# Pairwise addition of RMS-norm squares on VectorE, four square buffers, and norm steps spread over the output projection

## The chip, the cores and the metric

The kernel runs on the eight cores of one Trainium2 chip, each with two of the sixteen sequences and its own copy of the weights. No core waits for another. The metric is the device time in microseconds of the slowest core. The engines are named as in the profile: PE (TensorE, matmuls), DVE (VectorE), ACT (ScalarE), POOL (GpSimd) and SP (SyncE, which here only issues DMAs). PEld is PE's weight load.

## What is computed

A two-layer trunk on x of shape 16 x 2048 x 1024. Each layer has an RMS norm, a joint input projection to three causal mixers, an output projection with a residual addition, a second RMS norm and a SwiGLU feed-forward network (FFN). One more RMS norm ends the trunk.

```python
def rms_norm(x, g):                      # cut to what matters
    y = x * rsqrt(mean(x * x, axis=-1, keepdims=True) + 1e-6)
    return y * g

for l in range(2):
    h = rms_norm(x, norm1_g[l])
    z = h @ w_in[l]                       # 1024 -> 1792
    ya = conformer_conv(z[..., :768])     # gate, causal conv of 31, layer norm, silu, pointwise
    yb = spatial_gating(z[..., 768:1536]) # gelu, layer norm, 128x128 mixing in chunks of 128
    yc = multiscale_pool(z[..., 1536:])   # trailing means over 2, 4, 8, 16
    x = x + concat(ya, yb, yc) @ w_out[l]
    h = rms_norm(x, norm2_g[l])
    gate, up = split(h @ w_gate_up[l])    # 2 x 2816
    x = x + (silu(gate) * up) @ w_down[l]
return rms_norm(x, final_g)
```

## The kernel before

x lies transposed in SBUF for the whole sequence, as `xT`: 128 channels by 8 blocks k, by 2048 positions in float32. Work goes in four tiles j of 512 positions. Each core runs sequence 0, layers 0 and 1, then sequence 1, layers 0 and 1. For each layer: input projection `A` (8 groups of 8 matmuls a tile, results to DRAM `yd` and back as `y2`), `conv`, the gating and pooling parts, `PW` (pointwise projection, 3 groups of 3 matmuls a tile), `WO` (output projection, 8 groups of 8 matmuls a tile, each followed by a residual addition on DVE) and the `FFN`. The FFN works in four chunks of the hidden size; after gate and up groups come down groups, in the last chunk 4 matmuls each, tile after tile, with a residual addition on DVE behind each group (line 990).

**The norms.** There are 40: `r1` before the input projection (16), `r2` before the FFN (16), `rF` at the end (8). `norm_closures` (line 534) makes a list of small steps for one norm of one tile. Step k squares block k on ACT (`sq`) into one of two 16-bit buffers `sqr`, and issues for block k-2 four matmuls of `sqr` against a column of ones (`stat`), which sum over the channels into 4 columns of one PSUM bank. For `r1` it also makes `xb`, the scaled 16-bit copy, on DVE for even k and on ACT for odd k (`mkxb`). The last step, `fin`, reads the bank on DVE and takes the power -0.5 on POOL. After `r2`, `bcast_closures` spreads the result over the partitions (`dia` on DVE, one matmul) and eight DVE operations write `h2T`.

**What sets the order.** Each engine runs its queue in the order in which the program issues instructions. `push` puts a step into a queue `bg`, `tick(n)` takes n steps out of it, and `need(tag)` takes steps out until the tagged one is done. Ticks stand behind groups of matmuls: 1 behind each down group of the last chunk and each group of `A`, 5 behind each group of `WO`, 1 behind each of `PW`, 4 behind each gate or up group. `idle(n)` pushes n steps that issue nothing for the norm. At the start of a sequence `x_tr` transposes the input with one tick for each of 8 groups; `fin_store` does the same for the output of the sequence before. In the first sequence `band_consts`, which goes back and forth between POOL and DVE, is issued after the steps of tile 1's norm are pushed and before `A` takes them. In the layer that follows an FFN, the norms of tiles 0 to 2 run beside the last down groups of the next tile and what is left runs in `A`.

**Waits.** `Prog.add` derives waits from the buffers that each instruction names: a write waits for the earlier readers and writers of every buffer whose address range overlaps. `next_bank` gives the 8 PSUM banks in turn and passes over one that has been written and not yet read. From offset `AB` on lies a region of 134336 bytes in which tiles of different stages share addresses; `sgB` (offset 129216, 3072 bytes) holds the gate norm's constants, loaded on SP before `A` of tile 3.

Of the kernel before, what the change touches and what calls it, by code (L numbers as in the profile page):

```python
# [7 lines left out]
BF16 = mybir.dt.bfloat16  # L8
# [178 lines left out]
def build_program(nseq=2, depth=2):  # L187
# [109 lines left out]
    ybt = AT("ybt", 123072, [128, 4, DB], BF16)  # L297
    sgB = AT("sgB", 129216, [128, 2, DB], F32)
    ya = [AT("ya%d" % i, 110784 + 3072 * i, [128, 3, NT], BF16) for i in range(2)]
    cb32 = AT("cb32", 132288, [32, DA], BF16)  # L300
    cbf = AT("cbf", 124608, [32, DA], F32)
    cbr = AT("cbr", 126144, [32, DA], F32)
# [87 lines left out]
    def push(fn, tag=None, q=None):  # L390
        (bg if q is None else q).append((fn, tag))
# [37 lines left out]
    def bxT(k, j):  # L429
        return B("xT", k, j)  # L430
# [7 lines left out]
    def jc(j):  # L438
        return slice(j * NT, (j + 1) * NT)
# [94 lines left out]
    def norm_closures(s, l, j, rt, kind, with_xb):  # L534
        st = {}
        sqs = {}
        br = B("r", kind, j)

        def sq(k):
            i = sq_rr[0] % len(sqr)  # L540
            sq_rr[0] += 1
            sqs[k] = i
            act_op(sqr[i][:], xT[:, k, jc(j)], AF.Square, [bxT(k, j)], [B("sqr", i)])

        def stat(k):
            if k == 0:
                st["bk"], st["bb"] = next_bank()
            bk, bb = st["bk"], st["bb"]
            i = sqs[k]

            def fn(e, bk=bk, i=i, k=k):
                ins = None
                for q in range(4):
                    ins = e.matmul(bk[:, q:q + 1], sqr[i][:, q * 128:(q + 1) * 128], ocS[:, 0:1],  # L554
                                   start=(k == 0 and q == 0), stop=(k == 7), skip_group_check=True)
                return ins
            P.add("tensor", fn, reads=[B("sqr", i), bC], writes=[bb])

        def mkxb(k):
            if k % 2 == 0:  # L560
                ts(xb[j][:, k, :], xT[:, k, jc(j)], pvc(l, PV_G1 + k), None, ALU.mult, None, [bxT(k, j), bPV], [bxb(j, k)])
            else:
                act_op(xb[j][:, k, :], xT[:, k, jc(j)], AF.Copy, [bxT(k, j), bPV], [bxb(j, k)],
                       scale=pvc(l, PV_G1 + k))

        def fin():
            ts(rt[:, 4 * j:4 * j + 4], st["bk"][:, 0:4], RMS_EPS, None, ALU.add, None, [st["bb"]], [br])
            pool(lambda e: e.tensor_tensor(out=rt[:, 4 * j:4 * j + 4], in0=rt[:, 4 * j:4 * j + 4],  # L568
                                           in1=mhalf[:, 0:4], op=ALU.pow), [br, bC], [br])

        def step(k):
            if k >= 2:
                stat(k - 2)
            if k < 8:
                if with_xb:
                    mkxb(k)
                sq(k)
        for k in range(9):
            push(lambda k=k: step(k))

        def last():
            stat(7)
            fin()
        push(last, (kind, s, l, j))

    def idle(n):
        def other():
# [347 lines left out]
    def norm2(s, l, j):  # L935
        norm_closures(s, l, j, r2, "r2", False)
        hold = {}
        idle(5)

        def sink(bk, bb):  # L940
            hold["k"] = (bk, bb)
        bcast_closures(s, l, j, r2, "r2", sink)

        def sc(k):
            bk, bb = hold["k"]
            stt(h2T[j][:, k, :], xT[:, k, jc(j)], pvc(l, PV_G2 + k), bk[:], ALU.mult, ALU.mult,
                [bxT(k, j), bb, bPV], [bh2(j, k)])
        for k in range(8):
            push(lambda k=k: sc(k), ("h2", s, l, j) if k == 7 else None)
# [233 lines left out]
```

How the kernel before makes its waits and increments, by code:

```python
                def body(eh):  # L165
                    for fn, waits, tok, dma in e.ops:
                        for k, v in waits:
                            eh.wait_ge(sems[k], v)
                        ins = fn(eh)
                        ins.then_inc(sems[tok[0]], 16 if dma else 1)
                    if e.name == "sync":
                        for k, v in finals:
                            eh.wait_ge(sems[k], v)
```

## Time and profile before

| | |
|---|---|
| median of 3 runs | 3058.99 us (3058.8 to 3324.05) |
| profiled execution, slowest core | 3059.71 us |
| span of core 0 (profiled), first to last instruction | 3058.1 us |
| spans of cores 1 to 7 | 3019.6 to 3050.5 us |
| PE busy | 2844.7 us (93%), 15632 matmuls |
| DVE busy | 1207.3 us (39%) |
| ACT busy | 823.5 us (27%) |
| POOL busy | 177.4 us (6%) |
| mean granted PE clock, core 0 | 0.958 |

The profile is that of the slowest core. A busy share is an average over stages with different limits: PE is the bound almost everywhere, and the other engines matter where PE waits for them. In the rows below, a wait in brackets is the idle time of that engine just before the instruction, with what ended it. Matmuls are pipelined, so the busy time of short ones overlaps with that of their neighbours. Idle time of an engine that isn't the bound costs nothing.

### The profile page before, as it was taken

To read this page: it belongs to the slowest core of one execution; us is meant where nothing else is said; L and a number is where in the kernel's file an instruction comes from. 1 tells how busy PE (TensorE), PEld (TensorE's weight loads), DVE (VectorE), ACT (ScalarE), POOL (GpSimd) and SP (SyncE) were. 2 spreads that over 40 slices of the span, in tenths; PEclk is the share of its full clock that TensorE was granted. 3 is DMA by queue.
4 is the path that set the end of the run, shared out by engine and by line. 5 is a ranking of instruction groups with operands and counts; after the bars stand their busy time and mean duration, and the time that the engine had idled before them with its cause. 6 is when DMAs were issued, how large, how long until landed. Compare 5 with 4: busy or idle time off the path is not lost.

```text
span 3058.1 us, 44571 instructions; the slowest of 8 cores (3019.6 to 3058.1 us)
## 1 busy us (share of the span) xinstructions
PE 2844.7 (93%) x15632; PEld 1451.3 (47%) x15632; DVE 1207.3 (39%) x2108; ACT 823.5 (27%) x1356; POOL 177.4 (6%) x286
## 2 busy tenths in 40 slices
PE   5889999999997999999988889999999889999998
PEld 3554344444555444444465544444445544444444
DVE  2372422323554523223354633323335634223236
ACT  3544111010545220110255541010025442110102
POOL 2000000000001010000000001000000000000000
PEclk8887799999998999999998899999999899999999
DMA  8304062220131252221243034221003040222102
GB/s 188 53 1 70 3 94 38 42 32 14 25 53 23 48 83 35 42 36 31 74 151 76 8 63 65 52 42 35 14 15 60 17 69 4 39 41 43 29 21 111
DMA packets 123463, 148.44 MB, mean 49 GB/s; under 512 B 71664, under 2 KB 98416, under 8 KB 121200
## 3 DMA queue, kind: packets, MB, share of 16 engines
q0 software_dynamic: 37376, 100.80, 20.3%
q1 hardware_dynamic: 85872, 44.80, 5.5%
q8 instruction: 131, 2.15, 0.3%
q14 instruction: 84, 0.69, 0.1%
HBM read 219.12 MB, written 23.07 MB: 79 GB/s over the span
## 4 chain that ended last, share of the span: by engine, by line
PE 84%; DVE 6%; issue 4%; ACT 2%; DMA 2%; POOL 1%; SPq 1%; DVEq 0%; ACTq 0%; POOLq 0%
PE bank L332 78%; PE bank L350 2%; PE bank L726 2%; DVE bna L741 1%; ACT sqr L361 1%; PE bank L554 1%; DVE ybt L383 1%; DVE bnv L780 1%; DVE vn L383 1%; PE bank L720 1%; SPq L324 1%; DVE vg L383 1%; DMA yd<-ytok 1%; ACT silT L361 1%; POOL bna L746 1%
## 5 line engine op out<-in xcount | busy, mean ns | idle before, releaser
L332 PE MATMUL bank<-h2T,ring 128*128 128x512 bf16 x5632 | 1227.2, 380 | 0.0
L332 PEld LDWEIGHTS bank<-h2T,ring 128*128 128x128 bf16 x5632 | 551.5, 98 | 667.9 <-issue 22.6
L371 DVE TENSOR_TENSOR xT<-xT,bank 128x512 f32<-128x512 f32 x640 | 438.2, 687 | 506.2 <-PE bank L332 419.3
L332 PE MATMUL bank<-act,wd 128*128 128x512 bf16 x2816 | 618.1, 379 | 7.5 <-DVE r L377 3.7
L371 DVE TENSOR_TENSOR act<-tsil,bank 128x512 bf16<-128x512 f32 x352 | 242.2, 688 | 953.2 <-PE bank L332 945.4
L361 ACT ACTIVATE tsil<-bank 128x512 f32<-128x512 f32 x352 | 210.1, 597 | 1496.6 <-PE bank L332 1483.9
L332 PEld LDWEIGHTS bank<-act,wd 128*128 128x128 bf16 x2816 | 269.9, 98 | 323.4 <-issue 8.0
L361 ACT ACTIVATE sqr<-xT 128x512 bf16<-128x512 f32 x320 | 191.4, 624 | 207.3 <-PE bank L554 194.9
L332 PE MATMUL bank<-w_a_sb,xb 128*128 128x384 bf16 x1024 | 180.1, 336 | 12.9 <-DVE r L377 12.9
L332 PE MATMUL bank<-w_uv_sb,xb 128*128 128x384 bf16 x1024 | 184.0, 343 | 0.0
L332 PEld LDWEIGHTS bank<-w_uv_sb,xb 128*128 128x128 bf16 x1024 | 105.1, 103 | 78.2 <-issue 19.5
L332 PEld LDWEIGHTS bank<-w_a_sb,xb 128*128 128x128 bf16 x1024 | 99.8, 100 | 79.7 <-issue 22.1
L554 PE MATMUL bank<-ocS,sqr 128*128 128x1 bf16 x1280 | 72.4, 164 | 51.7 <-ACT sqr L361 49.5
L554 PEld LDWEIGHTS bank<-ocS,sqr 128*128 128x128 bf16 x1280 | 66.9, 97 | 97.6 <-issue 68.8
L332 PE MATMUL bank<-ybT,wo 128*128 128x512 bf16 x384 | 111.2, 401 | 0.0
L332 PE MATMUL bank<-ya,wo 128*128 128x512 bf16 x384 | 111.1, 401 | 0.0
L324 POOL DMA_DIRECT2D ring<-w_gate_up x88 | 46.7, 534 | 868.3 <-PE bank L332 823.0
L383 DVE SCALAR_TENSOR_TENSOR h2T<-xT,pv,bank 128x512 bf16<-128x512 f32 x128 | 86.6, 741 | 2.4 <-PE bank L332 2.4
L383 DVE SCALAR_TENSOR_TENSOR ytok<-bank,r,sig 128x384 bf16<-128x384 f32 x64 | 39.5, 618 | 119.8 <-PE bank L332 68.5
L332 PE MATMUL bank<-yc,wo 128*128 128x512 bf16 x256 | 81.4, 402 | 0.0
L568 POOL TENSOR_TENSOR r<-r,mhalf 128x4 f32<-128x4 f32 x32 | 32.8, 1024 | 679.0 <-DVE r L377 660.1
L741 DVE BATCH_NORM_STATS2 bna<-xc 128x6 f32<-128x384 f32 x64 | 50.4, 788 | 41.8 <-ACT xc L361 41.8
(123 smaller groups left out, 1762.0 us busy)
## 6 DMA issues: line engine op xcount, KB each, us to landing
ring<-w_gate_up POOLq DMA_DIRECT2D x88, 512.0 KB, 7.4
wd<-w_down POOLq DMA_DIRECT2D x12, 1536.0 KB, 12.1
xst<-x SPq DMA_DIRECT2D x24, 512.0 KB, 6.8
out<-osF SPq DMA_DIRECT2D x16, 512.0 KB, 4.3
w_a_sb<-w_a POOLq DMA_DIRECT2D x8, 768.0 KB, 16.3
w_uv_sb<-w_uv POOLq DMA_DIRECT2D x8, 768.0 KB, 27.0
yd<-ytok SPq DMA_DIRECT2D x16, 384.0 KB, 2.8
y<-yd SPq DMA_DIRECT2D x128, 48.0 KB, 2.9
```

The source lines that it names most:

```text
L324: return P.add(q, lambda e, out=out, in_=in_: e.dma_start(out=out, in_=in_), reads=reads, writes=writes, dma=True, final=final)
L332: ins = e.matmul(out, l, r, start=(first and i == 0), stop=(last and i == n - 1))
L350: ins = e.transpose(out, in_, idn)
L361: return e.activation(out=out, in_=in_, func=func, **kw)
L371: return P.add(eng, lambda e, out=out, in0=in0, in1=in1, op=op: e.tensor_tensor(out=out, in0=in0, in1=in1, op=op), reads=reads, writes=writes)
L383: e.scalar_tensor_tensor(out=out, in0=in0, scalar=scalar, in1=in1, op0=op0, op1=op1),
L554: ins = e.matmul(bk[:, q:q + 1], sqr[i][:, q * 128:(q + 1) * 128], ocS[:, 0:1], start=(k == 0 and q == 0), stop=(k == 7), skip_group_check ...
L568: pool(lambda e: e.tensor_tensor(out=rt[:, 4 * j:4 * j + 4], in0=rt[:, 4 * j:4 * j + 4], in1=mhalf[:, 0:4], op=ALU.pow), [br, bC], [br])
L720: e.matmul(bk[:], onesb[0:32, :], cb32[:, 32 * b:32 * b + 32].unsqueeze(2).to_broadcast([32, 32, TB]), start=True, stop=False, skip_group_ ...
L726: ins = e.matmul(bk[:, gp * 128:(gp + 1) * 128], y2[:, 2 - d:2 - d + NBLK, g], toep[:, g, d].rearrange("p i t -> p (i t)"), start=False, s ...
L741: vec(lambda e: e.bn_stats(out=bna[:, ti, 0:6], in_=xc[:, :, t]), allx, [bst[ti]])
L746: pool(lambda e: e.tensor_tensor(out=bna[:, :, 10], in0=bna[:, :, 10], in1=mhalf[:, 0:4], op=ALU.pow), bst + [bC], bst)
```

## The change

Squares go to four buffers `sqa`, which share addresses with `sgB` (three of them) and lie behind `cb32` (the fourth). For each pair p of blocks a DVE addition `add(p)` sums two square tiles into `sqr[p % 2]`, in 16-bit, and `stat(p)` sends this sum through the ones-column matmuls: 4 groups of four instead of 8 for each norm. A norm has 6 steps instead of 10. Step p issues `stat(p-2)`, then both copies and both squares of pair p, then `add(p-1)`; step 5 issues `stat(3)` and `fin`. For `r2`, an idle step stands behind each of the first five, and `norm2` pushes 4 idle steps instead of 5, so that the number of steps until the broadcast is the same, 15 either way.

```diff
--- before.py
+++ after.py
@@ -297,6 +297,7 @@
     ybt = AT("ybt", 123072, [128, 4, DB], BF16)
     sgB = AT("sgB", 129216, [128, 2, DB], F32)
     ya = [AT("ya%d" % i, 110784 + 3072 * i, [128, 3, NT], BF16) for i in range(2)]
+    sqa = [AT("sqa%d" % i, (129216, 130240, 131264, 133056)[i], [128, NT], BF16) for i in range(4)]
     cb32 = AT("cb32", 132288, [32, DA], BF16)
     cbf = AT("cbf", 124608, [32, DA], F32)
     cbr = AT("cbr", 126144, [32, DA], F32)
@@ -537,24 +538,27 @@
         br = B("r", kind, j)
 
         def sq(k):
-            i = sq_rr[0] % len(sqr)
+            i = sq_rr[0] % len(sqa)
             sq_rr[0] += 1
             sqs[k] = i
-            act_op(sqr[i][:], xT[:, k, jc(j)], AF.Square, [bxT(k, j)], [B("sqr", i)])
-
-        def stat(k):
-            if k == 0:
+            act_op(sqa[i][:], xT[:, k, jc(j)], AF.Square, [bxT(k, j)], [sqa[i].b()])
+
+        def add(p):
+            a, b = sqs[2 * p], sqs[2 * p + 1]
+            tt(sqr[p % 2][:], sqa[a][:], sqa[b][:], ALU.add, [sqa[a].b(), sqa[b].b()], [B("sqr", p % 2)])
+
+        def stat(p):
+            if p == 0:
                 st["bk"], st["bb"] = next_bank()
             bk, bb = st["bk"], st["bb"]
-            i = sqs[k]
-
-            def fn(e, bk=bk, i=i, k=k):
+
+            def fn(e, bk=bk, p=p):
                 ins = None
                 for q in range(4):
-                    ins = e.matmul(bk[:, q:q + 1], sqr[i][:, q * 128:(q + 1) * 128], ocS[:, 0:1],
-                                   start=(k == 0 and q == 0), stop=(k == 7), skip_group_check=True)
+                    ins = e.matmul(bk[:, q:q + 1], sqr[p % 2][:, q * 128:(q + 1) * 128], ocS[:, 0:1],
+                                   start=(p == 0 and q == 0), stop=(p == 3), skip_group_check=True)
                 return ins
-            P.add("tensor", fn, reads=[B("sqr", i), bC], writes=[bb])
+            P.add("tensor", fn, reads=[B("sqr", p % 2), bC], writes=[bb])
 
         def mkxb(k):
             if k % 2 == 0:
@@ -568,20 +572,22 @@
             pool(lambda e: e.tensor_tensor(out=rt[:, 4 * j:4 * j + 4], in0=rt[:, 4 * j:4 * j + 4],
                                            in1=mhalf[:, 0:4], op=ALU.pow), [br, bC], [br])
 
-        def step(k):
-            if k >= 2:
-                stat(k - 2)
-            if k < 8:
-                if with_xb:
-                    mkxb(k)
-                sq(k)
-        for k in range(9):
-            push(lambda k=k: step(k))
-
-        def last():
-            stat(7)
-            fin()
-        push(last, (kind, s, l, j))
+        def step(p):
+            if p >= 2:
+                stat(p - 2)
+            if p < 4:
+                for k in (2 * p, 2 * p + 1):
+                    if with_xb:
+                        mkxb(k)
+                    sq(k)
+            if 1 <= p <= 4:
+                add(p - 1)
+            if p == 5:
+                fin()
+        for p in range(6):
+            push(lambda p=p: step(p), (kind, s, l, j) if p == 5 else None)
+            if kind == "r2" and p < 5:
+                idle(1)
 
     def idle(n):
         def other():
@@ -935,7 +941,7 @@
     def norm2(s, l, j):
         norm_closures(s, l, j, r2, "r2", False)
         hold = {}
-        idle(5)
+        idle(4)
 
         def sink(bk, bb):
             hold["k"] = (bk, bb)
```

## Rows read from the trace of the kernel before

**Rows 1.** the page's chain of work that ended last, shares of the span

```profile
PE 84%; DVE 6%; issue 4%; ACT 2%; DMA 2%; POOL 1%; SPq 1%; DVEq 0%; ACTq 0%; POOLq 0%
```

**Rows 2.** groups by line: engine, what, count | busy us, mean ns | idle

```profile
L371 DVE TENSOR_TENSOR xT<-xT,bank 128x512 f32<-128x512 f32 x640 | 438.2, 687 | 506.2 <-PE bank L332 419.3 <-PE bank L554 86.6
L554 PE MATMUL bank<-ocS,sqr 128*128 128x1 bf16 x1280 | 72.4, 164 | 51.7 <-ACT sqr L361 49.5 <-issue 1.0 <-DVE xT L618 0.6
L361 ACT ACTIVATE sqr<-xT 128x512 bf16<-128x512 f32 x320 | 191.4, 624 | 207.3 <-PE bank L554 194.9 <-DVE xT L371 11.2 <-DVE r L377 1.0
```

**Rows 3.** timeline, FFN end of layer 0: start us, us, engine, what

```profile
789.83 0.24 PE L554 MATMUL bank<-ocS,sqr 128*128 128x1 bf16 x4
...
790.79 0.24 PE L554 MATMUL bank<-ocS,sqr 128*128 128x1 bf16 x4
...
797.75 2.75 PE L332 MATMUL bank<-act,wd 128*128 128x512 bf16 x12 [0.94 <-DVE r L377]
798.88 0.69 DVE L371 TENSOR_TENSOR xT<-xT,bank 128x512 f32<-128x512 f32 x1 [1.28 <-PE bank L332]
799.48 0.48 DVE L377 TENSOR_SCALAR xb<-xT,pv 128x512 bf16<-128x512 f32 x1
799.88 0.68 DVE L371 TENSOR_TENSOR xT<-xT,bank 128x512 f32<-128x512 f32 x1
800.33 0.24 PE L554 MATMUL bank<-ocS,sqr 128*128 128x1 bf16 x4
...
812.87 1.46 PE L332 MATMUL bank<-w_a_sb,xb 128*128 128x384 bf16 x8
```

**Rows 4.** timeline, FFN end of layer 1

```profile
1515.95 2.75 PE L332 MATMUL bank<-act,wd 128*128 128x512 bf16 x12 [0.94 <-DVE rF L377]
```

**Rows 5.** timeline, first sequence, norm of tile 3

```profile
89.31 1.14 ACT L361 ACTIVATE sqr<-xT 128x512 bf16<-128x512 f32 x2
90.35 0.72 ACT L361 ACTIVATE xb<-xT,pv 128x512 bf16<-128x512 f32 x1
...
90.96 0.62 ACT L361 ACTIVATE sqr<-xT 128x512 bf16<-128x512 f32 x1
91.73 0.24 PE L554 MATMUL bank<-ocS,sqr 128*128 128x1 bf16 x4 [0.88 <-ACT sqr L361]
```

**Rows 6.** timeline, output projection of layer 1, first sequence

```profile
1011.95 0.34 PE L554 MATMUL bank<-ocS,sqr 128*128 128x1 bf16 x8
1012.22 0.69 DVE L371 TENSOR_TENSOR xT<-xT,bank 128x512 f32<-128x512 f32 x1 [3.43 <-PE bank L554]
...
1014.29 0.81 PE L332 MATMUL bank<-ya,wo 128*128 128x512 bf16 x3
...
1016.22 0.81 PE L332 MATMUL bank<-ya,wo 128*128 128x512 bf16 x3
...
1049.22 0.34 PE L554 MATMUL bank<-ocS,sqr 128*128 128x1 bf16 x8
...
1054.57 0.81 PE L332 MATMUL bank<-ya,wo 128*128 128x512 bf16 x3
```

**Rows 7.** timeline, input projections with a norm beside them

```profile
821.10 4.06 PE L332 MATMUL bank<-w_a_sb,xb 128*128 128x384 bf16 x24 [0.42 <-DVE r L377]
...
1561.25 0.58 ACT L361 ACTIVATE sig<-bank,r 128x384 f32<-128x384 f32 x1
...
1569.71 0.64 PE L350 MATMUL bank<-identF,xT 128*128 128x128 f32 x4
```

**Rows 8.** timeline, first sequence, tile 1 behind the band constants

```profile
57.88 0.19 DVE L371 TENSOR_TENSOR bandc<-bt,bandc 128x32 bf16<-128x32 f32 x1
...
59.83 0.48 PE L332 MATMUL bank<-w_a_sb,xb 128*128 128x384 bf16 x1 [11.28 <-DVE r L377]
```

**Rows 9.** busy by stretch: stretch, us, PE, PEld, DVE, ACT, POOL, clock, DMA

```profile
1552.00:1562.00 10.00, 9.24 (x47) 7.49 (x48) 3.14 (x7) 3.82 (x6) 1.01 (x1) 0.66 0.35 117
...
1008.00:1016.20 8.20, 6.63 (x57) 3.34 (x56) 1.38 (x2) 5.97 (x11) 0.00 (x0) 1.00 0.74 147
```

## Prediction

> **What bounds the kernel now.** I read the page's chain of work first. PE carries 84% of it [rows 1], so a microsecond taken from PE is a microsecond of the end, and one added in front of PE is too. The other engines count only where PE waits for them. Then the groups of instructions by line: the change works on the squares of the RMS norms, 320 on ACT and 1280 one-column matmuls on PE, four for each square, and there PE waits 49.5 us for ACT [rows 2]. The busy time of those matmuls (72.4 us) overstates them, so I read their price in the timeline. At the end of an FFN a step of the last down projection with a group of four takes 0.96 us from one group of four to the next (789.83 to 790.79); without it three steps take 797.75 to 800.33, 0.86 each [rows 3]. A group of four costs PE 0.10 us.
>
> Three other things are in the timeline. Each norm that goes on beside one matmul group per step leaves a wait "<-DVE r" of 0.94 us: the norm's PSUM bank comes round again just when the norm ends [rows 3, 4]. In the output projection PE stands between two groups (1011.95 to 1014.29), because with two buffers each square waits for an older square's matmuls [rows 6]. And at the start of a sequence the squares are bound by ACT itself: two squares 1.04 us apart from the copy behind them, the copy another 0.61, so 1.65 us a pair [rows 5].
>
> **What the change takes away.** 160 of the 320 groups of four go: 160 x 0.10 = 16 us of PE. The norm holds its bank for four steps instead of eight, so the 0.94 us waits at the FFN ends go too: two at each of four ends, 7.5 us. Four square buffers let ACT run ahead.
>
> **What it adds.** 160 additions on VectorE, and with each a wait: the matmuls of pair p are issued one step after the addition, and the addition stands in DVE's queue behind the residual addition of its step, which waits for that step's PE work. No addition of two 16-bit tiles is in the trace. From below stands the 0.48 us scaling that writes a 16-bit tile of the same shape, whose successor starts 0.40 us later (799.48 to 799.88); from above the 687 ns residual addition from PSUM, whose successor starts 0.60 us later (798.88 to 799.48) [rows 2, 3]. I take 0.48 and 0.40: operands in SBUF and a 16-bit result are nearer to the first; both ends are kept.
> The row nearest by operation is the 687 ns one; the Trainium skill, VectorE: DVE Perf Modes, "The TRN2 errata", gives such a float32 addition (N+151)/0.96, 691 ns at 512, with which that row agrees, and "The perf-mode tier table" lets an addition of 16-bit tiles in SBUF run at twice the rate, which would be an estimate of 424 ns. No row here shows that; by it the whole sum would be 2 us smaller.
>
> **FFN ends of layer 0 (twice).** Count from the end of the down group that pushes the norm. A residual addition starts 0.27 us behind its group's end (1011.95 to 1012.22), the next DVE work 0.60 later, the scaling takes 0.40, the addition 0.48, and PE starts about 0.15 behind its releaser (90.96 + 0.62 to 91.73) [rows 5, 6]. Step 0: residual 0.27, scaling 0.87, free at 1.27. Step 1 (group ends 0.86): residual 1.27, scaling 1.87, addition 2.27 to 2.75. Step 2's group ends at 1.72, but its matmuls can't start before 2.90: PE stands 1.2 us. From there DVE needs 0.60 + 0.40 + 0.40 = 1.40 us a step and PE 0.96, and PE is tied to it: the next three matmul groups start at 4.3, 5.8 and 7.0, waits of 0.4, 0.5 and 0.3. ACT doesn't set this: squares 0 to 3 are done before, squares 4 and 5 start at 2.85 and 6 and 7 end by 6.3, which moves only the last addition. Then three bare steps; eight take 9.7 us. Before, group 2 at 789.83 to the first matmuls of layer 1 at 812.87 gives 23.04 us for 22 steps; with the two before it 24.7 for 24, 8.25 per eight [rows 3]. Three norms: +4.4, two ends: **+8.8**. The 7.5 us of bank waits and half of the groups are already in this.
>
> **FFN ends of layer 1 (twice).** No scaling there, DVE needs 1.00 a step. The same walk gives waits of 0.6, 0, 0.5 and 0 and 8.5 us per eight steps, against the same period before (the wait of 0.94 is there too [rows 4]): 0.25 x 6 = **+1.5**.
>
> **Input projections with a norm beside them.** Before, one square goes with each 8-matmul group (1.35 us, 24 matmuls in 4.06). Now two squares and one scaling, 1.65 us of ACT, fall on one group, with the sigmoid (0.5) between. In layer 0 of the second sequence the first sigmoid, behind the table load, ends at 1561.83, so square 1 ends at 1563.5 and its addition at 1564.1; the first matmuls, for which PE is there at 1562.6, start at 1564.2, and the later ones wait for squares 3, 5 and 7, 0.2, 0.7 and 0.25. The next transposes come at 1572.4 instead of 1569.71 [rows 7]: +2.8. For the next tile, without a table load, the same gives +1.75. In layer 1 squares 2 and 3 stand behind that table load: the sixth group starts at 9.75 after the first, where 812.87 to 821.10 are 8.2 [rows 3, 7], and after what later groups save +1.3, twice: **+2.6**. The yd DMA and the convolution are behind these, so nothing hides them.
>
> **Start of the first sequence.** Tile 1's norm is issued behind the band constants, where DVE is blocked by GpSimd until 57.88. Before, only four scalings waited there while ACT and PE did squares and matmuls, and tile 1's projection began at 59.83 [rows 8]. Now the additions wait too, and squares 4 to 7 wait for their buffers: first addition 58.8 to 59.3, squares 4 and 5 until 61.1 (two squares and a copy between them), squares 6 and 7 until 62.8, last addition 63.4, projection 63.6: +3.8. Tiles 0 and 3 (exposed, ACT-bound [rows 5]) get one addition and one hand-over more, 0.6 each; tile 2, beside the transposes of tile 3, one ACT pause more, about 1.0. **+6.0**. Start of the second sequence: the 2.8 and 1.75 above, 0.6 for tile 3's norm, 0.5 for additions among the final scalings of stores: **+5.7**. End of the kernel, DVE-bound on output scalings: four additions, 1.6, less a bank wait that goes: **+0.6**.
>
> **Output projection.** The step spread is meant for the stand of [rows 6]. Tiles 0 and 1: the first group of four and its wait leave, PE is at 1011.6. Pair 1's addition waits for square 3 (ACT until 1012.4) and the residual addition, then is done at 1013.0; matmuls 1013.1, next group 1013.2 to 1015.0. Pair 3's addition stands behind the next residual: 1015.8 to 1016.3, next group 1016.5, where it was 1016.22: +0.3 each. Tile 2: 1049.22 to 1054.57 before; now its two stalls are 1.4 and 1.2 and it ends 0.4 earlier. Tile 3, in the FFN, 0.35 earlier. Per block -0.15, four blocks **-0.6**. One wait goes, another of the same length comes: the residual addition is late next.
>
> **Sum.** 8.8 + 1.5 + 2.6 + 6.0 + 5.7 + 0.6 - 0.6 = 24.6 us. The profiled execution took 3059.71 us (span 3058.1), the median is 3058.99, so I set it on the median: **3083.6 us**. No DMA is added or moved; the constants for the gate's norm share addresses with the square buffers, and their loads on SP come after the last square there, so I give that nothing (if not, SP's y loads behind them are late by an addition).
>
> **Rivals.** (a) *Faster.* Every addition is done when its matmuls come; then PE keeps the 16 us and the 7.5 us: 3059.0 - 23.5 = 3035.5. It holds from the point at which residual, scaling and addition end inside the next step, 1.0 us after the group; the rows make it 0.27 + 0.60 + 0.40 + 0.48 + 0.15 = 1.9 with the scaling and 1.5 without. For it speaks DVE's low load, against it the queue's order. 0.15. (b) *The addition is as slow as the residual one* (0.69, next after 0.60): 0.2 us more at each wait, 0.8 x 6 + 0.6 x 6 + 1.3 x 4 + 1.5 = 15 us: 3098.6. 0.10. (c) *The clock.* From 1552 to 1562, behind a wait for a norm's bank, the granted clock is 0.66 [rows 9]: part of it at 1.2 GHz, part at 2.4. If the new waits of 1.6 us in four input projections do that, each loses up to 3.4: +13.6, 3097.2. A wait of 2.3 us in the output projection left it at 1.00 [rows 6, 9], which speaks against. 0.10.
> The Trainium skill, TensorE: Matmul & The Clock Gate, "HAM oscillation", says that idle gaps in PE's work bring the clock back to half; [rows 9] agree, the output projection doesn't.
> (d) *The parts cancel*: small waits are absorbed by banks I counted as tied: 3059. 0.05. The forecast: 0.60, own range 3070 to 3097.
>
> **Range and chances.** To leave out no more than 2 in 10: from 3045 (most of (a) outside) to 3100 ((b) and (c) inside). About 2% is what this measurement can tell from no change, 61 us here; no case reaches it: same 0.97, faster 0.02, slower 0.01.
>
> **What would show it.** The changed profile should have 640 one-column matmuls, 160 additions of about 0.48 us, PE waits "<-DVE sqr" at every FFN end of layer 0 (1.2 then about 0.4), no 0.94 us wait "<-DVE r" there, tile 1's first projection near 63.6, and two waits of over a microsecond per norm in the output projection. It is wrong if additions run ahead of the residual ones, or if ACT, not DVE, releases PE at the FFN ends.

## The result: 0.6% slower, and the profile after

| | before | after |
|---|---|---|
| median | 3061.13 us (13 runs) | 3077.09 us (13 runs) |
| time against before | | 1.0059, interval 1.0036 to 1.0081 |
| profiled execution, slowest core | 3059.71 us | 3077.09 us |
| mean span of the eight cores, profiled | 3039.1 us | 3061.0 us |
| PE busy, slowest core | 2844.7 us | 2823.2 us |
| DVE busy, slowest core | 1207.3 us | 1266.3 us |

The change costs 11 to 25 us (the interval times 3060), most likely 18. The medians are of all 13 runs; ratios, intervals and means over several runs, here and below, leave out runs in which the cores of a die were held at a lower clock throughout. PE is busy for 21.5 us less and is done later. The page's chain of work that ended last, and four groups by line (columns as in [rows 2]):

```profile
PE 79%; DVE 8%; issue 5%; ACT 3%; DMA 2%; POOL 1%; SPq 1%; DVEq 0%; ACTq 0%; POOLq 0%
...
L372 DVE TENSOR_TENSOR xT<-xT,bank 128x512 f32<-128x512 f32 x640 | 438.5, 687 | 452.1 <-PE bank L333 412.7
L362 ACT ACTIVATE sqa<-xT 128x512 bf16<-128x512 f32 x320 | 183.2, 619 | 161.6 <-DVE sqr L372 116.4
L558 PE MATMUL bank<-ocS,sqr 128*128 128x1 bf16 x640 | 38.1, 164 | 112.8 <-DVE sqr L372 112.6
L372 DVE TENSOR_TENSOR sqr<-sqa,sqa 128x512 bf16<-128x512 bf16 x160 | 66.4, 421 | 53.8 <-ACT sqa L362 49.6
```

PE's share of the chain fell from 84% [rows 1] to 79%, and DVE's rose from 6 to 8. The one-column matmuls are halved, but PE's idle time in front of them rose from 51.7 us [rows 2] to 112.8, nearly all of it behind the addition. ACT, which waited 194.9 us for PE, now waits 116.4 us for the addition to free a square buffer.

The end of an FFN of layer 0 on core 2 of after (timeline: start us, us, engine, line, what, [idle before <- releaser]):

```profile
784.36 0.48 DVE L378 TENSOR_SCALAR xb<-xT,pv 128x512 bf16<-128x512 f32 x1
784.75 0.42 DVE L372 TENSOR_TENSOR sqr<-sqa,sqa 128x512 bf16<-128x512 bf16 x1
785.09 0.68 DVE L372 TENSOR_TENSOR xT<-xT,bank 128x512 f32<-128x512 f32 x1
...
785.32 0.24 PE L558 MATMUL bank<-ocS,sqr 128*128 128x1 bf16 x4 [0.94 <-DVE sqr L372]
...
786.65 0.24 PE L558 MATMUL bank<-ocS,sqr 128*128 128x1 bf16 x4 [0.21 <-DVE sqr L372]
...
788.11 0.24 PE L558 MATMUL bank<-ocS,sqr 128*128 128x1 bf16 x4 [0.34 <-DVE sqr L372]
...
789.48 0.24 PE L558 MATMUL bank<-ocS,sqr 128*128 128x1 bf16 x4 [0.24 <-DVE sqr L372]
```

Where [rows 3] had a group of four every 0.96 us and one wait of 0.94 for the norm's bank, four groups now stand behind DVE, each at the end of residual, scaling and addition. The addition takes 0.42 us, and its successor on DVE starts 0.34 us after it (784.75 to 785.09).

The start of the first sequence on core 2, behind the band constants [rows 8]:

```profile
57.03 0.19 DVE L372 TENSOR_TENSOR bandc<-bt,bandc 128x32 bf16<-128x32 f32 x1
...
57.97 0.41 DVE L372 TENSOR_TENSOR sqr<-sqa,sqa 128x512 bf16<-128x512 bf16 x1
...
58.63 0.24 PE L558 MATMUL bank<-ocS,sqr 128*128 128x1 bf16 x4 [17.96 <-DVE sqr L372]
...
62.70 0.25 PE L558 MATMUL bank<-ocS,sqr 128*128 128x1 bf16 x4 [1.41 <-DVE sqr L372]
```

The start of the second sequence on core 0 (timeline):

```profile
1528.84 1.41 DVE L384 SCALAR_TENSOR_TENSOR osA<-bank,rF,gFB 128x512 f32<-128x512 f32 x2 [4.70 <-DMA out<-osA]
...
1529.73 1.29 PE L351 MATMUL bank<-identF,xst 128*128 128x128 f32 x8 [2.97 <-DVE osA L384]
...
1552.49 0.24 PE L558 MATMUL bank<-ocS,sqr 128*128 128x1 bf16 x4 [2.08 <-DVE sqr L372]
...
1560.67 3.66 PE L351 MATMUL bank<-identF,xT 128*128 128x128 f32 x32
...
1571.79 2.73 DVE L384 SCALAR_TENSOR_TENSOR osB<-bank,rF,gFB 128x512 f32<-128x512 f32 x4 [7.52 <-DMA out<-osB]
...
1572.68 3.64 PE L351 MATMUL bank<-identF,xst 128*128 128x128 f32 x16 [6.61 <-DVE osB L384]
```

To see where the time went I took the starts of the stages on PE from the timelines of all eight cores of both profiled executions:

| stage, medians over cores, us | before | after | difference |
|---|---|---|---|
| start to the first projection | 25.0 | 25.5 | +0.5 |
| input projection, sequence 1 layer 0 | 103.5 | 109.8 | +6.3 |
| input projection, sequence 2 layer 0 | 97.3 | 104.0 | +6.7 |
| input projections, layer 1 (two) | 57.3, 57.6 | 57.9, 58.8 | +0.6, +1.2 |
| output projections (four) | 74.9, 76.7, 73.5, 73.4 | 73.9, 73.9, 73.8, 73.8 | -1.0, -2.8, +0.3, +0.4 |
| FFN of layer 0 (two) | 463.5, 463.4 | 467.9, 467.8 | +4.4, +4.4 |
| FFN of layer 1 with the stores behind it | 488.6 | 492.5 | +3.9 |
| last FFN of layer 1 and the last stores | 492.2 | 492.1 | -0.1 |
| convolution, gating, pooling (four) | 122.7, 120.2, 119.1, 122.2 | 124.0, 120.5, 119.5, 121.3 | +1.3, +0.3, +0.4, -0.9 |

The stage that the change does not touch (the last line of the table) varies by up to 10 us from core to core (118.5 to 129.1 in before), so a single pair of executions is good to some 5 us: the mean spans of this pair differ by 22.0 us, those over several runs by 14.7 (3057.5 over ten runs of after; 3042.8 over the 21 runs of before that e1 to e4 were compared with).

### The profile page after: what moved, and what is told of

It is laid out like the page before. It is cut to its first block, busy times and chain, and to the rows that moved or that the text cites. A ratio compares the mean times of both kernels' runs of the same rounds, so it can differ in the third digit from the quotient of the medians.

```text
span 3074.9 us, 43068 instructions; the slowest of 8 cores (3049.6 to 3074.9 us)
## 1 busy us (share of the span) xinstructions
PE 2823.2 (92%) x14992; PEld 1426.7 (46%) x14992; DVE 1266.3 (41%) x2268; ACT 819.4 (27%) x1356; POOL 177.6 (6%) x286
## 4 chain that ended last, share of the span: by engine, by line
PE 79%; DVE 8%; issue 5%; ACT 3%; DMA 2%; POOL 1%; SPq 1%; DVEq 0%; ACTq 0%; POOLq 0%
PE bank L333 73%; PE bank L351 2%; PE bank L732 2%; ACT sqa L362 2%; DVE bna L747 1%; DVE sqr L372 1%; DVE ybt L384 1%; DVE bnv L786 1%; SPq L325 1%; DMA yd<-ytok 1%; DVE vn L384 1%; PE bank L726 1%; PE bank L558 1%; PE bank L894 1%; DVE xT L372 1%
## 5 line engine op out<-in xcount | busy, mean ns | idle before, releaser
L362 ACT ACTIVATE sqa<-xT 128x512 bf16<-128x512 f32 x320 | 183.2, 619 | 161.6 <-DVE sqr L372 116.4
L558 PE MATMUL bank<-ocS,sqr 128*128 128x1 bf16 x640 | 38.1, 164 | 112.8 <-DVE sqr L372 112.6
L558 PEld LDWEIGHTS bank<-ocS,sqr 128*128 128x128 bf16 x640 | 31.5, 97 | 155.3 <-issue 149.7
L372 DVE TENSOR_TENSOR sqr<-sqa,sqa 128x512 bf16<-128x512 bf16 x160 | 66.4, 421 | 53.8 <-ACT sqa L362 49.6
## 6 DMA issues: line engine op xcount, KB each, us to landing
wd<-w_down POOLq DMA_DIRECT2D x12, 1536.0 KB, 12.6
```

The source lines that it names most:

```text
L362: return e.activation(out=out, in_=in_, func=func, **kw)
L372: return P.add(eng, lambda e, out=out, in0=in0, in1=in1, op=op: e.tensor_tensor(out=out, in0=in0, in1=in1, op=op), reads=reads, writes=writes)
L558: ins = e.matmul(bk[:, q:q + 1], sqr[p % 2][:, q * 128:(q + 1) * 128], ocS[:, 0:1], start=(p == 0 and q == 0), stop=(p == 3), skip_group_c ...
```

## The experiments

My theory: PE loses time because the addition stands in DVE's queue behind the residual addition of its own step, and its matmuls come one step later. Rivals: the addition itself is too slow, the four buffers or the spread steps do it, or the clock.

All runs beside the kernel before; us are (ratio - 1) x 3060. Line numbers in the fences are each kernel's own.

| kernel | ratio | interval | us |
|---|---|---|---|
| after | 1.0059 | 1.0036 to 1.0081 | +18 |
| four buffers, no addition (e1) | 0.9919 | 0.9887 to 0.9951 | -25 |
| one square a step (e2) | 1.0008 | 0.9975 to 1.0040 | +2 |
| residual addition behind the steps (e3) | 0.9986 | 0.9957 to 1.0015 | -4 |
| no spread (e4) | 1.0153 | 1.0111 to 1.0195 | +47 |
| additions twice (e5) | 1.0251 | 1.0224 to 1.0279 | +77 |
| band constants later (e6) | 1.0066 | 1.0030 to 1.0101 | +20 |
| best places, band later (e7) | 0.9881 | 0.9860 to 0.9902 | -36 |
| e1 with band later (e8) | 0.9933 | 0.9907 to 0.9958 | -21 |
| best places, band in place (e9) | 0.9842 | 0.9823 to 0.9861 | -48 |
| best places, band early (e10) | 0.9805 | 0.9786 to 0.9823 | -60 |
| e10 without the addition (e11) | 0.9848 | 0.9823 to 0.9874 | -47 |

**e1, the buffers alone.** The kernel before, with its squares in the four `sqa` (the matmuls read them there; cut):

```diff
-            i = sq_rr[0] % len(sqr)
+            i = sq_rr[0] % len(sqa)
-            act_op(sqr[i][:], xT[:, k, jc(j)], AF.Square, [bxT(k, j)], [B("sqr", i)])
+            act_op(sqa[i][:], xT[:, k, jc(j)], AF.Square, [bxT(k, j)], [sqa[i].b()])
```

> The kernel before with four square buffers and nothing else: 320 squares, 1280 one-column matmuls, ten steps, no addition. Queue theory (PE stands where the order of the queues makes it wait, and nothing else counts): in the output projection ACT no longer waits for PE's matmuls of an older square, so tiles 0 and 1 lose 0.6 us of their stand each, tile 2 about 2.7, tile 3 about 1.3: 5 us a block, 20 us in all, ratio to before 0.9935; the waits of 0.94 us for DVE's r at the FFN ends stay. Rival (the four buffers are of no use by themselves, since ACT is idle most of the time and the gain lies in halving the matmuls): within 4 us of before, 1.000.

It measured 25 us faster than before. The group of one-column matmuls on its page, and its output projection on core 0:

```profile
L555 PE MATMUL bank<-ocS,sqa 128*128 128x1 bf16 x1280 | 69.0, 164 | 34.7 <-ACT sqa L362 31.6
...
1001.75 0.24 PE L555 MATMUL bank<-ocS,sqa 128*128 128x1 bf16 x4 [0.25 <-ACT sqa L362]
1002.27 0.24 PE L555 MATMUL bank<-ocS,sqa 128*128 128x1 bf16 x4 [0.28 <-ACT sqa L362]
```

The stand of [rows 6] is down to waits of 0.3 us, and a block (the output projection of one layer) takes 70.0 us instead of 73.4 or 76.5. So of the change's parts the buffers are worth -25 us, and the additions with the new steps +43 on top of them.

**e5, the addition doubled.** Each addition is issued twice, with the same result.

> The changed kernel with every addition issued twice into the same tile (320 additions; the second waits for the first). It measures how tightly PE is tied to them: each pair's sum is 0.5 us later. Queue theory (each of the 104 waits for DVE's sums grows by most of it): 30 to 45 us above the changed kernel, ratio to before 1.018. Rival (DVE is busy for 41% and has room): 5 us or less above it, 1.007.

59 us more than after for 67 us more of DVE's work (160 x 0.42), where I had expected 30 to 45. The FFN end of layer 0 on core 3:

```profile
785.89 0.24 PE L559 MATMUL bank<-ocS,sqr 128*128 128x1 bf16 x4 [1.47 <-DVE sqr L372]
...
787.75 0.24 PE L559 MATMUL bank<-ocS,sqr 128*128 128x1 bf16 x4 [0.73 <-DVE sqr L372]
...
789.61 0.24 PE L559 MATMUL bank<-ocS,sqr 128*128 128x1 bf16 x4 [0.74 <-DVE sqr L372]
```

Each wait grew by 0.4 to 0.53 us: PE is tied to DVE's queue there. The last wait before the norm's end grew less, 0.24 to 0.34. Part of what came on top of my 45 us is the clock: in a layer 0 FFN on core 0 the granted clock of after stays at 1.00, while in e5 it falls to 0.50 twice (at 346.6 and at 797.2), and in 22 of the 32 blocks of e5 it falls too, in none of after but those of cores 2 and 3 in one layer.

**e3, the order in DVE's queue.** The steps are taken before the residual addition is issued, at the FFN ends and in the output projection (this is the edit in the output projection):

```diff
-            tt(xT[:, n, jc(j)], xT[:, n, jc(j)], bk[:], ALU.add, [bxT(n, j), bb], [bxT(n, j)])
             tick(5)
+            tt(xT[:, n, jc(j)], xT[:, n, jc(j)], bk[:], ALU.add, [bxT(n, j), bb], [bxT(n, j)])
```

> The changed kernel with one order turned round: in the last down projection and in the output projection the steps of the norm are issued ahead of the residual addition of their matmul group, so an addition of squares no longer stands behind the residual addition of its own step. Queue theory: at the FFN ends of layer 0 the first wait of 0.94 us goes and eight steps take 8.0 to 8.3 us instead of 9.7 (9 us less in all), at those of layer 1 3 us less, in the output projection the waits behind the residual addition (1.2 us, two a norm for tiles 0 to 2) go for the most part, 4 to 5 us a block: 28 to 32 us below the changed kernel, ratio to before about 0.996. Rival (ACT's squares, not DVE's queue, release PE): within 4 us of the changed kernel.

22 us faster than after, the intervals apart; expected were 28 to 32. The FFN end on core 0:

```profile
781.78 0.24 PE L558 MATMUL bank<-ocS,sqr 128*128 128x1 bf16 x4
...
783.11 0.24 PE L558 MATMUL bank<-ocS,sqr 128*128 128x1 bf16 x4 [0.21 <-DVE sqr L372]
...
784.44 0.24 PE L558 MATMUL bank<-ocS,sqr 128*128 128x1 bf16 x4 [0.21 <-DVE sqr L372]
...
786.01 0.24 PE L558 MATMUL bank<-ocS,sqr 128*128 128x1 bf16 x4 [0.45 <-DVE sqr L372]
```

The wait of 0.94 is gone. The others stay, because DVE's 1.3 us of work a step (residual, scaling, addition) don't fit into PE's 0.96. In all the four FFNs are 10 us shorter (465.8, 465.4, 489.5 and 489.3 us in the medians, after 467.9, 467.8, 492.5 and 492.1). In the output projection the second wait of each norm is gone, since its addition no longer stands behind a residual addition that waits for PE. A block takes 68.1 to 69.9 us in 18 of 32 cases, after 73.9, which would be 22 us for four. The other 14 take 76.3 to 78.9 us, at a lower granted clock. The same block on cores 0 and 4:

```profile
1000.00:1070.00 70.00, 67.97 (x296) 28.70 (x294) 40.40 (x69) 18.90 (x34) 3.04 (x3) 0.81 0.19 32
...
970.00:1037.00 67.00, 62.31 (x318) 28.77 (x323) 41.63 (x72) 19.21 (x35) 3.05 (x3) 1.00 0.32 53
```

So the order is worth about the 30 us that I expected where the clock holds, and some of it was lost to the clock; why it fell on these cores, no run shows.

**e2, one square a step.** The pace of the kernel before (10 steps), a sum in every second step, and its matmuls two steps behind it. No spread over the output projection.

> The changed kernel with the pace of the kernel before: one square a step, ten steps, the addition of a pair in its second step, its matmuls two steps later, no spread in the second norm. The additions are the same 160. Queue theory: two steps between addition and matmuls are 1.8 us, about the 1.9 that residual addition, scaling and addition need, so the waits at the FFN ends shrink to under 0.2 each and eight steps take 7.4 us instead of 9.7: 14 us less than the changed kernel there, 8 less in the input projections and their neighbours, 0 to 4 less in the output projection: 22 to 28 us below the changed kernel, ratio to before 0.997. Rival (the additions cost what they take of DVE, 160 x 0.4 us, wherever they stand): as the changed kernel, 1.006 to before.

16 us faster than after (the intervals just overlap; expected were 22 to 28), level with before. No wait is left at the FFN ends (a layer 0 FFN takes 462.8 us against 467.9). So the second half of the cause is that the change puts 1.3 us of DVE work into a step of 0.96 and has PE need the sum one step later; e2 turned both round together, and no run tells them apart. Without the spread the output projection waits, and on core 0 it then slows down. Core 0 and, from 989.03, core 2 of the same execution:

```profile
989.58 0.24 PE L558 MATMUL bank<-ocS,sqr 128*128 128x1 bf16 x4 [1.28 <-DVE sqr L372]
990.76 0.24 PE L558 MATMUL bank<-ocS,sqr 128*128 128x1 bf16 x4 [0.94 <-DVE sqr L372]
...
993.11 1.44 PE L333 MATMUL bank<-ya,wo 128*128 128x512 bf16 x3
...
989.03 0.24 PE L558 MATMUL bank<-ocS,sqr 128*128 128x1 bf16 x4 [0.94 <-DVE sqr L372]
989.00:994.00 5.00, 4.97 (x31) 2.40 (x32) 2.23 (x5) 0.25 (x1) 1.03 (x1) 1.00 0.00 0
```

Three matmuls take 1.44 us on core 0, 0.81 in [rows 6], and the granted clock of 991 to 996 is 0.66. On core 2 the waits are the same, 1.28 and 0.94 us, and the granted clock stays at 1.00 (last line, columns as in [rows 9]). The waits alone don't decide it.

**e4, the spread alone.** After, without the idle steps between those of `r2`; nine come behind them instead of four, so that the broadcast stays in its place.

```diff
-            if kind == "r2" and p < 5:
-                idle(1)
 ...
-        idle(4)
+        idle(9)
```

> The changed kernel without the spread of the second norm over the output projection: its six steps one behind the other, then nine idle ones, so that the broadcast comes at the same place. Queue theory: the spread takes a wait of one length for another; without it three groups of four wait at one place for squares 3, 5 and 7, 0.5 us a norm more for tiles 0, 1 and 3, nothing for tile 2: 5 us above the changed kernel, ratio to it 1.002. Rival (the spread is what saves the stand of 2.3 us in the output projection): 20 us or more above the changed kernel.

The miss of the study: 29 us over after, where I had expected 5. The waits of a norm add up to 3.0 us against 2.7 in after, so they are little of it. The matmuls behind them are most. Its output projection on core 0, and its busy time by stretch (columns as in [rows 9]):

```profile
1002.25 0.24 PE L558 MATMUL bank<-ocS,sqr 128*128 128x1 bf16 x4 [1.11 <-DVE sqr L372]
...
1005.52 0.24 PE L558 MATMUL bank<-ocS,sqr 128*128 128x1 bf16 x4 [1.20 <-DVE sqr L372]
1006.47 0.24 PE L558 MATMUL bank<-ocS,sqr 128*128 128x1 bf16 x4 [0.71 <-DVE sqr L372]
...
1007.21 1.35 PE L333 MATMUL bank<-ybT,wo 128*128 128x512 bf16 x3
...
1006.50:1014.00 7.50, 7.50 (x29) 3.00 (x30) 2.44 (x5) 0.00 (x0) 1.03 (x1) 0.77 0.00 0
```

The same stretches in after, on core 0, and in before, on core 2:

```profile
995.00:1003.00 8.00, 5.23 (x38) 2.67 (x38) 3.15 (x7) 5.24 (x11) 0.14 (x1) 1.00 0.43 72
1003.00:1012.00 9.00, 8.95 (x40) 3.88 (x40) 6.94 (x11) 0.00 (x0) 0.89 (x1) 1.00 0.01 2
```

```profile
1010.00:1020.00 10.00, 8.54 (x56) 3.92 (x55) 2.46 (x5) 4.82 (x9) 1.01 (x1) 0.83 0.01 2
```

In e4 the granted clock is at 2.4 GHz until the waits are over (1.00 from 998 to 1006.5), partly at 1.2 GHz in the stretch behind them (0.77 on average), and back at 2.4 after it. It falls a second time at 1048.3, but not behind the waits of the norm in between (1.18, 1.20 and 0.65 us, 1024.65 to 1028.80). In after, with 1.51 and 1.20 us of waiting 3.3 us apart, it stays at 2.4. In before it falls in some blocks: 10 of the 30 blocks that nothing else disturbed took 76.4 to 76.8 us, the other 20 73.2 to 73.6, behind the same waits. After has none: all 30 lie at 73.8 to 74.0. Every block of e4 on core 0 takes 78.5. So this is what the spread is worth in the output projection, 4.6 us a block, 18 us in all; about 3 of the 4.6 are the clock, by what two falls cost a block of before. The rest is in the FFN, where the norm of tile 3 ends: a layer 0 FFN takes 471.7 us against 467.9, with waits of 1.43 and 1.93 us in place of one of 1.54, and a third fall of the clock behind them (at 1072.2). The four FFNs give 15 us, and the 33 in all is what the mean spans of the two profiled executions differ by (3093.8 and 3061.0).

**e6, the band constants.** `band_consts()` is issued behind the input projection of tile 1 instead of in front of it.

> The changed kernel with the band constants issued behind the input projection of tile 1. If the additions of tile 1's norm were late because DVE stood behind these constants, that projection starts at about 49 us instead of 62.8, and the kernel is 14 us faster than the changed one (ratio to before 1.001); in the kernel before the same move is worth 11. Rival (they waited for ACT's squares): 3 us or less.

Nothing gained (the intervals of e6 and after overlap), against 14 us expected. Core 7:

```profile
49.03 12.48 PE L333 MATMUL bank<-w_a_sb,xb 128*128 128x384 bf16 x64
...
77.72 0.19 DVE L372 TENSOR_TENSOR bandc<-bt,bandc 128x32 bf16<-128x32 f32 x1
77.83 2.48 DVE L624 COPY xT<-bank 128x512 f32<-128x512 f32 x4
...
78.66 1.94 PE L351 MATMUL bank<-identF,xst 128*128 128x128 f32 x8 [10.06 <-DVE xT L624]
```

Tile 1's projection starts 14 us earlier (the median over the cores is 49.4 us, in after 63.5), as intended. But the constants now stand in front of the copies of tile 2, and PE waits 8.4 to 12.4 us there, depending on the core. The wait was moved, not removed.

**e8.** The same move on e1, without any addition.

> The kernel before with four square buffers, no addition, and the band constants issued behind the input projection of tile 1. Both theories: the wait of 11.2 us in front of tile 1's projection goes, since DVE gets to that norm's scalings and its fin at once: 36 us below the kernel before, ratio 0.988. What it tells apart is the next run's cause: how much of that run's gain is the band constants and the buffers alone, and how much the additions with a fitting order.

No gain either (-21 us, e1 -25, intervals overlap): it isn't the additions that make the move useless.

**e7, the best places.** Sums two steps ahead of their matmuls, one square a step for `r1` and `rF`, two idle steps between those of `r2`, the residual addition behind the steps, the band constants as in e6.

> A version with 160 additions in which no queue order should make PE wait: norms beside the FFN ends and the input projections at the old pace (one square a step, matmuls two steps behind their addition), the second norm in six steps three apart, the steps ahead of the residual addition, and the band constants issued behind the input projection of tile 1. Queue theory: FFN ends of layer 0 as in the run with one square a step (about 1 us under before), the output projection of a layer at 64 to 66 us where before has 73.5 to 76.8, 11 us less at the start of the first sequence: 45 to 55 us below the kernel before, ratio 0.983. Rival (the additions have a price of their own, 160 x 0.4 us of DVE, whatever their place): not faster than the run with four buffers alone, 0.992.

36 us faster than before, 54 faster than after; expected were 45 to 55 below before. Its FFN end of layer 0 on core 0 has no wait left:

```profile
774.34 0.24 PE L558 MATMUL bank<-ocS,sqr 128*128 128x1 bf16 x4
774.44 1.89 PE L333 MATMUL bank<-act,wd 128*128 128x512 bf16 x8
776.16 0.24 PE L558 MATMUL bank<-ocS,sqr 128*128 128x1 bf16 x4
```

A layer 0 FFN takes 460.4 or 459.9 us (before 463.5), a block of the output projection 66.5 to 67.4. The 11 us that I had counted for the start of the first sequence did not come, as in e6.

**e9, the band constants back.**

> The kernel of e7_two_steps_apart with the band constants back in their place of the kernel before. That run had them later, and in e6 the later place brought nothing, because VectorE's small operations on them stood ahead of the copies of tile 2 (a wait of 12.4 us there in place of one of 18). If the place of the band constants is worth nothing, this run measures as e7 did, ratio 0.988 (0.985 to 0.991). If e7 owed part of its gain to it, this run is 10 to 15 us slower, 0.992 to 0.993.

It came out faster than e7, not slower, but the mean spans of all cores in the compared runs are the same (2994.7 us both; those of the befores beside them 3038.7 and 3041.0), so most of the difference lies in how far the slowest core stood out. The place of the band constants is worth nothing that these runs can tell, as long as they hold DVE.

**e10, the band constants taken apart.** GpSimd's part goes to the kernel's start, and so does VectorE's arithmetic on four small tables, now apart in memory. Eight small operations stay at the old place. The part for the tables, cut:

```diff
+    for g, w in enumerate((2, 4, 8, 16)):
+        pool(lambda e, g=g: e.iota(bt4[:, g, :], [[1, 32]], base=1, channel_multiplier=0,
+                                   allow_small_or_imprecise_dtypes=True), [], [bt4.b()])
+    for g, w in enumerate((2, 4, 8, 16)):
+        ts(bt4[:, g, :], bt4[:, g, :], float(w), None, ALU.min, None, [bt4.b()], [bt4.b()])
+        vec(lambda e, g=g: e.reciprocal(out=bt4[:, g, :], in_=bt4[:, g, :]), [bt4.b()], [bt4.b()])
+        ts(bt4[:, g, :], bt4[:, g, :], 1.0 / w, None, ALU.subtract, None, [bt4.b()], [bt4.b()])
```

> As e9, but the band constants are taken apart: GpSimd makes its part (12 us) in the first 25 us of the kernel, VectorE works on the four small tables before the first copy of x, where it is idle for 14 us, and only eight small operations of 0.18 us (1.5 us) stay at the old place, with nothing to wait for. Theory 1 (the wait of 11 to 18 us at the start is VectorE held up by its ping-pong with GpSimd): the wait falls to about 3 to 6 us and the kernel is 10 to 13 us faster than e9, ratio 0.984. Rival (TensorE would wait there anyway, for the additions or the copies of tile 1, or GpSimd's early work delays a load): 0 to 3 us, ratio 0.987 to 0.988.

The fastest kernel, 2994.45 us in the median. First core 4 of e9, then core 1 of e10:

```profile
59.44 0.24 PE L558 MATMUL bank<-ocS,sqr 128*128 128x1 bf16 x4 [17.91 <-DVE sqr L372]
```

```profile
45.72 0.24 PE L564 MATMUL bank<-ocS,sqr 128*128 128x1 bf16 x4 [3.91 <-ACT sqa L363]
...
49.91 12.19 PE L334 MATMUL bank<-w_a_sb,xb 128*128 128x384 bf16 x64
```

The wait of 17.91 us is one of 3.91, on every core within 0.02, and its releaser is ACT. Against e9 the kernel is 11 us faster (the intervals just touch; mean spans 2981.8 and 2994.7 us, 13), as the first theory said.

**e11, no addition.** The places of e10 with eight squares going straight to the matmuls.

> The four square buffers, the steps ahead of the residual addition, the spread over the output projection and the early band constants of e10, but without the addition: eight squares go to eight groups of ones-column matmuls. It tells what the addition itself is worth once its steps lie well. e10 against it: 320 fewer groups of ones-column matmuls (72.4 us of TensorE before, 38.1 after, so up to 34 us less work) against the waits that the addition brings at the starts of both sequences (about 1.4 us a norm step there). Theory 1 (the addition pays where norms are hidden): e11 is 10 to 20 us slower than e10, ratio about 0.989. Rival (buffers and places give the whole gain, and the matmuls saved lay in waits anyway): within 5 us of e10, ratio 0.984 to 0.986.

13 us slower than e10 in the ratio and 12.6 in the mean spans (2994.4 against 2981.8); the intervals just touch, over four and three runs, so the 13 is good to about 10. Waits for the norm's bank are back at e11's FFN ends (0.42 us <-DVE r, none in e10). So a pairwise addition does pay, by about 13 us, where I had counted 16 for the matmuls and 7.5 for the bank waits, once DVE has it ready in time. Of the 60 us of e10, 47 come without it.

## Why the prediction was right

The forecast was 24.6 us slower, measured were 18 (11 to 25), and the mechanism is the one forecast. That the sum came so near is in part luck: the start of the second sequence cost 4.6 us more than its term, and the output projection, the input projections of layer 1 and the end of the kernel about 4 less. By its steps:

**What the change takes away.** Right. A group of four takes 0.10 us of PE (785.32 to the next matmul at 785.42), PE's busy time fell, and no "<-DVE r" wait is left at the FFN ends. e11 against e10 puts what the addition brings, with its sums in time, at 13 us.

**The cost of an addition.** 0.42 us and 0.34 to the successor, where I took 0.48 and 0.40. The estimate of 424 ns by the rate in the Trainium skill, VectorE: DVE Perf Modes, "The perf-mode tier table", was nearer: the group's mean is 421 ns.

**FFN ends of layer 0.** +8.8 forecast, +8.8 measured. Eight steps took 9.67 us (785.32 to 794.99) against 9.7. The waits in brackets, 0.94, 0.21, 0.34 and 0.24, look shorter than the 1.2, 0.4, 0.5 and 0.3 of the forecast, but they count from the modelled end of the matmuls, 1.02 us behind their start, where the next group can follow 0.86 us behind it [rows 3]. By the starts PE stood about 1.1, 0.37, 0.50 and 0.41 us (786.65 - 785.32 - 0.96 and so on), as forecast. e3 and e2 show both halves of the cause: the order (the first wait), and the load of a step with the lead of its sum (the other three).

**FFN ends of layer 1.** Waits 0.42, 0, 0.32, 0 and 8.36 us a period, forecast 8.5. From the FFN's start to the first transposes, core 0 needs 463.8 us against 463.5: +0.3 each, forecast +0.75 less 0.35 for tile 3 in the FFN.

**Input projections of layer 1.** Sixth group 9.74 us after the first on core 2, forecast 9.75; but later groups saved nearly all of it: when the next projection, that of the gating part, starts, only about 0.1 us is left (44.83 us after the first group against 44.68 to 44.75, on all cores). The +1.8 for two in the table, forecast +2.6, is mostly the time before the convolution, which varies from 1.4 to 5.1 us between cores in both kernels, so this term was too large.

**Start of the first sequence.** Tile 1's projection began at 63.4 us on core 0, forecast 63.6 (62.8 to 65.7 on the eight cores); the stage +6.3, with 0.5 before it, forecast +6.0.

**Start of the second sequence.** The term that was mis-sized: +5.7 forecast. The input projection alone brought +6.7 (5.15 forecast), and the stores before it about +3.6 (3.9 for the stage less 0.3), where I had put 0.5 for additions among the final scalings. On core 0 the first tile's groups took 14.3 us (1546.35 to 1560.67) against 11.8 (1557.90 to 1569.71). Behind them, 12.0 to 12.4 us pass in both kernels until DVE has `osB` (1560.67 to 1572.68; 1569.71 to 1582.13 before): projections, then on SP's queue the y loads and the stores of `osB`. What the norm saves in that stretch is saved inside a wait. In the first stores the norm ends earlier, and a scaling then waits 4.70 us for the DMA from `osA`, where before PE had only 0.2 us of such waits: I had counted every matmul taken away there as time won. And the clock fell in these stores, after on core 0 and before on core 0:

```profile
1531.00:1544.00 13.00, 10.71 (x63) 9.34 (x62) 11.04 (x21) 7.37 (x14) 1.01 (x1) 0.50 0.47 187
```

```profile
1531.00:1552.00 21.00, 15.85 (x193) 14.46 (x191) 15.76 (x28) 16.00 (x29) 2.04 (x2) 1.00 0.67 231
```

Behind the wait of 2.97 us at 1529.73 PE ran at 1.2 GHz until 1544.6. In before that came later and was shorter (1552.0 to 1558.8). PE's busy time at the lower clock, times the share that is missing, is 4.6 us in this FFN and the stores behind it in after and 1.4 in before (means of eight cores), so by this estimate the clock is 3 of the 3.6 us. That the stores and the clock take it back is read from these rows, and no run tested it alone.

**Output projection.** The waits are as forecast: two a norm, 1.51 and 1.20 us, and a block in which the clock holds in both kernels took 0.3 to 0.55 us more, forecast -0.15. What I missed is the clock in the kernel before. I had looked at one block, at 1.00 [rows 9], and took it for all; 10 of 30 blocks lost about 3 us each behind their waits. After loses none, and so the four blocks gave -3.1 us in the medians, -0.6 forecast.

**End of the kernel.** From the first transposes to the end of the span core 0 takes 29.6 us against 28.5, forecast +0.6. Over the eight cores the medians are 28.4 and 28.7, in a scatter of 27.7 to 29.7, so nothing can be told.

**The rivals.** (a) needs the addition done inside the next step; the 1.9 us against 1.0 were the right test, and e7 shows what it gives when it is met. (b) fell with 421 ns; e5 prices it, 59 us over 160 additions, 0.37 us of PE for each 0.42 us of DVE, the falls of the clock included. (c), as I put it, did not come: behind the new waits in the input projections (2.08 us at 1552.49, 1.63 at 807.54 on core 0) the granted clock of after is 1.00. But the clock is in the result all the same, in the stores before the second sequence, which I had not named, and in the blocks of e4. The Trainium skill, TensorE: Matmul & The Clock Gate, "HAM oscillation", has idle gaps in PE's work bring the clock back to half, and I had held the output projection against it. The trace of e4 agrees with that, at 0.77 behind three waits; those of after and of core 2 of e2 don't, at 1.00 behind two. (d) falls with the interval.

That the sum (24.6) lies at the upper end of the interval has no single cause that I can show: the second sequence's start cost about 5 more than forecast, the output projection, the input projections of layer 1 and the end about 4 less. The stage medians of the profiled pair add up to 25.9 and its mean spans differ by 22.0, while the means over several runs differ by 15. The rest is the scatter of single executions.

## What to carry to other kernels

Work moved off the bound engine pays only if the engine that takes it has it ready when the bound engine arrives: look at what stands in front of it in that engine's queue, and whether one step's work there fits into one step of the bound engine. Here the same 160 additions, with the steps that came with them, cost 43 us placed behind the residual additions with two squares a step (after against e1), and gained about 13 us placed ahead of them with two steps to spare (e10 against e11). And price each part of such a change alone: the buffers were worth 25 us and were hidden under the rest.

A long wait is best read as "who holds the queue": the band constants stopped costing only when they left DVE's queue at a busy time, not when their call was moved.

## What the runs showed of the hardware

- Waits of 0.3 to 1.3 us each, close together, can be followed by a stretch at 1.2 GHz, and the same waits are not always: 1.28 and 0.94 us, 1.2 us apart, were on core 0 of e2 (0.66) and were not on core 2 of it (1.00); 0.77 and 0.35 us, 1.1 us apart, were in 10 of the 30 undisturbed blocks of before; 1.11, 1.20 and 0.71 us within 5 us were at one norm of e4 (0.77, three matmuls in 1.35 us instead of 0.81), and nearly the same waits of the next norm were not. With 1.51 and 1.20 us, 3.3 us apart, no undisturbed block of after had one. What else decides it, these runs don't show.
- An addition of two 16-bit tiles of 128x512 in SBUF takes 421 ns on DVE, the addition from PSUM in float32 687.
- In some executions two neighbouring cores ran a stretch at a granted clock of 0.81, in before for most of 223 to 382 us on cores 0 and 1. A block of the output projection that lay in it took 11 to 16 us more (89.8 us on these cores, 84.5 on cores 2 and 3 of after, against 73.3 and 73.9). It is in both kernels, and in 14 of the 32 blocks of e3, so the slowest core of an execution isn't always slow for a reason in the kernel.
